# A block pair in fp32r on one core: the split weights get padded rows in place of two fixed offsets

## The reference

```python
h = modulate(rms_norm(x, pre_norm_mix), shift_m, scale_m)
o = attention(h @ w_in)                      # 2048 x 5656
x = x + gate_m * rms_norm(o @ w_o, post)     # 2048 x 2048
f = jnp.square(jax.nn.relu(h @ w_up)) @ w_down        # 2048 x 8192, 8192 x 2048
x = x + gate_f * rms_norm(f, post)
# second block: u @ w_in_2, three mixers, gates, branches, @ w_out_2, then
hdn = jnp.square(jax.nn.relu(_rms_norm(x, g) @ w_mlp_up))
x = x + _rms_norm(hdn @ w_mlp_down, post)
```

## Time and profile before

| | |
|---|---|
| median of 3 runs | 2995.68 us (2993.14 to 2997.9) |
| the profiled execution | 2997.9 us, span 2995.8 us |
| TensorE busy | 2902.8 us, 97% |
| VectorE busy | 1667.4 us, 56% |
| ScalarE busy | 1280.2 us, 43% |
| DMA | 596.72 MB, mean 199 GB/s |

### The profile page before, as it was taken

One profiled execution on the slowest core, in us unless ns is written; L12 is line 12 of the kernel. 1 busy time (PEld: TensorE's weight loads), 2 busy tenths in 40 slices (PEclk: granted clock), 3 DMA queues, 4 the chain that ended last, 5 costly groups with the idle time before them and its releaser, 6 DMA issues.

```text
span 2995.8 us, 50952 instructions
## 1 busy us (share of the span) xinstructions
PE 2902.8 (97%) x22340; PEld 2667.4 (89%) x22340; DVE 1667.4 (56%) x1484; ACT 1280.2 (43%) x1210; POOL 133.4 (4%) x111
## 2 busy tenths in 40 slices
PE   6999989999999999999999999999999999999999
PEld 5999987899889997889999789999978998899887
DVE  7878877794444454454455654444745444444444
ACT  3334444445334443346354444443344443344433
POOL 0011110000000000000022320000000000000000
PEclk8899999999999999999999999999999999999999
DMA  9998778596556655545451015556554555555553
GB/s 359 390 314 292 269 237 284 191 365 216 186 194 190 192 194 182 193 168 183 148 180 48 10 44 183 192 189 222 183 183 141 196 193 187 192 191 193 183 187 122
DMA packets 300452, 596.72 MB, mean 199 GB/s; under 512 B 12144, under 2 KB 17776, under 8 KB 299760
## 3 DMA queue, kind: packets, MB, share of 16 engines
q1 hardware_dynamic: 294864, 587.83, 58.1%
q10 hardware_dynamic: 5408, 6.23, 0.8%
HBM read 583.80 MB, written 6.29 MB: 197 GB/s over the span
## 4 chain that ended last, share of the span: by engine, by line
PE 86%; DVE 7%; ACT 3%; DMA 2%; issue 2%; POOL 0%; SPq 0%; ACTq 0%; DVEq 0%
PE ps L2275 32%; PE ps L2228 26%; PE ps L2791 9%; PE ps L2375 3%; PE ps L2390 3%; DVE ada_acc L1483 2%; PE ps L2912 2%; PE ps L2671 2%; DVE wL L1325 2%; ACT wH L765 1%; PE ps L2351 1%; DMA ada<-w_ada 1%; PE ps L2470 1%; ACT sqx L869 1%; PE ps L2252 1%
## 5 line engine op out<-in xcount | busy, mean ns | idle before, releaser
L1325 DVE TENSOR_TENSOR wL<-raw,wH 128x2048 fp32r<-128x2048 f32 x436 | 1004.3, 2304 | 1126.9 <-ACT wH L765 1122.5
L765 ACT ACTIVATE wH<-raw 128x2048 fp32r<-128x2048 f32 x436 | 837.3, 1920 | 1269.0 <-PE ps L2228 463.2
L2275 PE MATMUL ps<-actH,wH 128*128 128x256 f32 x2816 | 779.8, 277 | 2.9 <-DVE wL L1325 2.9
L2275 PE MATMUL ps<-actH,wL 128*128 128x256 f32 x2816 | 778.3, 276 | 0.0
L2275 PE MATMUL ps<-actL,wH 128*128 128x256 f32 x2816 | 778.3, 276 | 0.0
L2275 PEld LDWEIGHTS ps<-actH,wH 128*128 128x128 f32 x2816 | 529.5, 188 | 5.2 <-DVE wL L1325 3.3
L2275 PEld LDWEIGHTS ps<-actL,wH 128*128 128x128 f32 x2816 | 529.5, 188 | 0.1
L2275 PEld LDWEIGHTS ps<-actH,wL 128*128 128x128 f32 x2816 | 529.4, 188 | 0.0
L2228 PE MATMUL ps<-wL,hidH 128*128 128x512 f32 x1024 | 405.3, 396 | 0.0
L2228 PE MATMUL ps<-wH,hidH 128*128 128x512 f32 x1024 | 402.5, 393 | 1.3 <-DVE wL L1325 1.3
L2228 PE MATMUL ps<-wH,hidL 128*128 128x512 f32 x1024 | 401.0, 392 | 0.0
(11 more groups left out here) (419 smaller groups left out, 3681.5 us busy)
## 6 DMA issues: line engine op xcount, KB each, us to landing
raw<-w_in SPq DMA_DIRECT2D x96, 1024.0 KB, 5.2
ada<-w_ada SPq DMA_DIRECT2D x80, 1024.0 KB, 8.1
raw<-w_up SPq DMA_DIRECT2D x64, 1024.0 KB, 5.4
raw<-w_down SPq DMA_DIRECT2D x64, 1024.0 KB, 5.1
raw<-w_mlp_up SPq DMA_DIRECT2D x64, 1024.0 KB, 5.2
raw<-w_mlp_down SPq DMA_DIRECT2D x64, 1024.0 KB, 5.0
raw<-w_gates SPq DMA_DIRECT2D x48, 1024.0 KB, 5.1
raw<-w_o SPq DMA_DIRECT2D x16, 1024.0 KB, 6.2
```

The lines of the kernel that those rows point to most:

```text
L765: nc.scalar.activation(wH[:, s % SPLIT if L[name]["spg"] > 1 else r % SPLIT, :, :], raw[:, slot, :, :], ACT.Copy).then_inc(wh_ready, 1)
L1325: nc.vector.tensor_tensor(wL[:, b, :, :], raw[:, slot, :, :], wH[:, b, :, :].bitcast(F32), ALU.subtract).then_inc(wl_ready, 1)
L2275: ins = nc.tensor.matmul(out, w[:, b, k, cols], v[:, kk, :], start=(kk == 0 and j == 0 and n % 2 == 0), stop=(kk == STEP_K * spg - 1 and j ...
```

## The change

The two fixed offsets go. wH and wL get rows of `GC + PAD` = 516 elements, of which the first 512 are used: the rows of one block then lie 2064 bytes apart, not 2048. hidH, hidL, `o` and the scratch tiles behind it lie at whole KB from R0. Everything moves up by 96 bytes, and R0 is counted from the end of SBUF. Nothing else changes: instructions, their order, their waits and the bytes that they move are the same, but for the access patterns on wH and wL, which have four rows of 512 elements where there was one run of 2048.

```diff
-HIGH_AT, LOW_AT = 64, 192
+PAD = 4
...
-    top = [16512]
+    top = [16608]
...
     raw = new("raw", [P, RAW, STEP_K, GC])
-    top[0] += HIGH_AT
-    wH = new("wH", [P, SPLIT, STEP_K, GC], F32R)
-    top[0] += LOW_AT - HIGH_AT
-    wL = new("wL", [P, SPLIT, STEP_K, GC], F32R)
+    SPLIT0 = top[0]
+    wH = new("wH", [P, SPLIT, STEP_K, GC + PAD], F32R)[:, :, :, 0:GC]
+    wL = new("wL", [P, SPLIT, STEP_K, GC + PAD], F32R)[:, :, :, 0:GC]
...
-    R0 = ACT0 + 215 * 512
+    R0 = 229368 // 32 * 32 - 84 * 1024
...
-    hidH = at("hidH", [P, HT, T], F32R, R0 + HIGH_AT)
-    hidL = at("hidL", [P, HT, T], F32R, R0 + 32 * 1024 + LOW_AT)
-    o = at("o", [P, TT, D], F32, R0 + 64 * 1024 + LOW_AT)
+    hidH = at("hidH", [P, HT, T], F32R, R0)
+    hidL = at("hidL", [P, HT, T], F32R, R0 + 32 * 1024)
+    o = at("o", [P, TT, D], F32, R0 + 64 * 1024)
...
-    sqo = at("sqo", [P, TT, GC], F32, R0 + 80 * 1024 + LOW_AT)
+    sqo = at("sqo", [P, TT, GC], F32, R0 + 80 * 1024)
...
-    hid = at("hid_sq", [P, GT * T], F32, R0 + 80 * 1024 + LOW_AT)
+    hid = at("hid_sq", [P, GT * T], F32, R0 + 80 * 1024)
...
-    rtop[0] += LOW_AT
+    rtop[0] += 64 * PAD
```

## The result

| | before | after |
|---|---|---|
| median | 2996.51 us (2993.14 to 2997.9) | 3051.52 us (3044.9 to 3052.51, 4 runs) |
| profiled execution | 2997.9 us, span 2995.8 | 3041.57 us, span 3039.6 |

The ratio is 1.018, with a 95% interval of 1.0163 to 1.0198: the kernel is slower by 55 us. The forecast was no change, 2995 us, with 3025 as the upper end.

A forecast was written before the change was run, and what follows sets the result against it. TensorE's matmul pace was taken to bound the kernel. From the profiled 2997.9 us, -2.1 + 1.8 + 0 gave 2997.6, or 2995.4 on the median's scale; forecast 2995.0, no change, range 2963 to 3025.

The forecast's parts named there:

- What bounds the kernel: TensorE's matmul-to-matmul pace in the big-weight lines is the kernel's time: 2455 us of the 2996.
- VectorE and ScalarE at 0: The two splits per step, now four rows with gaps: a row break costs 0, and any cost is hidden.
- bound of 144 ns per row break: Splits on VectorE and ScalarE: a break costs at most an instruction start; three breaks 0.43 us, both engines 0.86.
- Transfers at 0: 1 MB loads land at another 256-byte phase; no cost in the sum, DMA share of the first 150 us unchanged.
- slower rival by transfers: DMA-full first 150 us: 2048-byte pieces may cost 96 bytes' worth more, 4.7%, +7 us, 3002; chance 0.05.
- Hidden activations at -2.1 us: Long matmuls with hidH and hidL stationary go from 231.1 to 230.4 ns, 3,072 of them: -2.1 us.
- The faster rival: 512-column matmuls lose their unevenness through 16-byte steps, all at 225 ns: -23 us, 2972; chance 0.26.
- Short matmuls at +1.8 us: 256-column matmuls: a third of 13,824 slow by 0.4 ns, the 0.3% of the nearest 512-column row: +1.8 us.
- The slower rival: 256-column matmuls slow where weights and activations share an address class: 4,608 at +4.4 ns, +20 us, 3015; chance 0.26.
- upper bound, +61 us: All short matmuls at 117.8 ns, the pace of the first ones behind a wait: +61 us, 3056.
- The sign in the profile after: L2275 pieces of 1536 at 177 us or more if the slower rival holds, more in wH products than wL.
- The rule on independent ports: TensorE has separate moving and weight-load read ports and never waits on another engine; by it distances are worth nothing.

The follow-up runs named there:

- e1: Kernel before with everything moved up by 96 bytes, distances between buffers unchanged: 2992.18 us against 2992.53, ratio 0.9999.
- e4: Kernel before with hidH and hidL alone moved to distance 0 from act: 2993.97 us, ratio 1.0004.
- e3: Kernel before with both offsets 0 and no padding, so wH, wL, hidH and hidL at distance 0 from act: 3057.71 us, ratio 1.0221.
- e8: Kernel before with wL and hidL moved to 64, so wH, wL, hidH and hidL all at 64: 3003.06 us, ratio 1.0036.
- e7: Kernel before with wL at distance 128 from act in place of 192, hidL kept at 192: 3055.21 us (one run) beside 2993.73.
- e2: Kernel before with only the wH and wL rows padded by 4 elements (16-byte steps), old offsets and base: 3053.82 us, ratio 1.021.
- e11: Kernel before with only a wait added ahead of up_1 and up2_1: 2992.21 us (one run), kernel before 2991.67.
- e9: Kernel before with hidL alone moved from 192 to 64: 2999.20 us against 2991.67, ratio 1.0023.
- e6: Kernel before with wL at distance 64 from act in place of 192, hidL kept at 192: 3014.19 us (one run) beside 2993.73.
- e10: e8 with a wait added ahead of up_1 and up2_1: 2993.58 us, ratio 1.0 to the kernel before.
- e5: Kernel before with wH and wL rows padded by one element (4-byte steps), old offsets: 3046.96 us (one run) against 2993.73.

## Why the prediction was wrong

- **What bounds the kernel: right.** TensorE's pace in the lines of the big matrices is its time, and the loss is made of 4.5 ns on each short matmul. TensorE's waits for a split stayed at 2.6 us ahead of L2274.
- **VectorE and ScalarE at 0: right.** The splits take 2306 and 1918 ns on four rows with gaps; before, the page has 2304 and 1920. The bound of 144 ns per row break was not needed.
- **Transfers at 0: right.** 1.01 and 1.03 busy at 356 and 380 GB/s in the first 150 us, and up_0 starts 0.5 us earlier than before. In e1 `raw` takes that phase of 224 with nothing padded, and the time is the same (0.9999): the slower rival by transfers did not happen.
- **Hidden activations at -2.1 us: right alone, not in the change.** Their move gives 230.4 ns (e4), but with stepping rows the long ones stay at 231.1 (177.49 us), so the term came out as 0. The faster rival, long ones at 225 ns through 16-byte steps, did not happen; what does bring them to 226.7 is distance 0 for all three products and no steps (e3, e8).
- **Short matmuls at +1.8 us: this is the step that failed.** I priced distances that no row showed by the nearest row, the 0.3% of the long form. The term took 0.4 ns on a third of the 13,824. The runs showed 4.5 ns, 4%, as the mean of all of them: 52.7 us on the 11,712 behind 560 us, of which 46.5 reach the chain. Two errors made that: the long form was taken to speak for the short one, while at distance 0 the one is fastest and the other slowest (e3); and 64 and 192 were read as two samples that see no sensitivity. They are the one sequence tried here that always falls to the fast pace; all at 0, wL at 128 and rows that step by 4 or 16 bytes hold it off, the last on most rows.
- **The slower rival: its place and its price for one matmul were right, its count was not.** Weights and activations at certain distances do slow the short stream, to about the 117.8 ns of the earlier trace rows. That this price fitted is not all luck: the nine matmuls behind a wait were the slow pace, seen before the stream fell out of it. The rival charged it to 4,608 matmuls (half the wH rows in two products), +20 us and 3015. e7 shows that one product at a bad distance slows all three, and e2 that good rows between bad ones are not clean. The prediction's upper bound, +61 us for all of them, 3056, was nearly the result of 3051.5. The range ended at 3025, short of a bound that the prediction had itself worked out for half of the span.
- **The sign in the profile after.** The prediction looked for more in the wH products than in the wL one. It rose in all of them (281, 281, 280 ns); e7 shows the same, one bad product slowing all three.
- **The rule on independent ports.** The prediction set the Trainium skill, "SBUF — State Buffer", section "Who interferes with whom", beside the rows: two independent read ports, and TensorE never waits on another engine. No run here shows TensorE waiting for another engine on account of an address, and its pace in e3 is 120.0 ns with VectorE and ScalarE busy or idle, so on that the trace agrees. Taken as far as the prediction took it, that distances between its two operands are worth nothing, the measurements decide against it: 113.4, 118.2 and 120.0 ns for the same instructions.

What is open: why the pace follows the distance. That it is counted modulo 256 is my measure and not shown: in every layout without stepping rows wH and wL lie a whole multiple of 512 bytes plus the given distance behind actH and actL, so the short stream never told 256 and 512 apart. Distances like 16, 32 or 48 were never tried without stepping rows. And actH and actL lie in one class, so that the short stream can't tell whether the distance to a matmul's own weights counts or that to the weights loaded for the next. Whether the moving read and the weight load of the next matmul meet in one place of SBUF, or whether it is something else, no run here tells. Nor is it shown which property of the entry picks the pace at 64 and 64. That front parts differ by some us between kernels with one pace of the short matmuls or nearly so, which hides gains of 5 us, is seen (the first x768 starts at 741.82 to 748.76 in before, e1, e4 and e8 to e11) and not explained.

## What to carry to other kernels

Where a stream of matmuls sets the time, its pace can hang on the addresses of both operands; measure it from a long stretch divided by its count, before and after anything that moves a buffer, padding of rows above all. Don't price an untested layout by another form of the same instruction; where no row covers the layout that half of the span will have, the range has to reach to the bound. If a stream runs above its best pace, try the other offsets below 256 bytes and a gap ahead of it, one at a time.

## What the runs showed of the hardware

At the 2.4 GHz level, for fp32r matmuls with a weight load each. Distances are those of the three products in their order in the stream:

| form | distances | ns each | seen in |
|---|---|---|---|
| 256 columns | 64, 64, 192 | 113.4 | before, e1, e4, e9, e11 |
| 256 columns | 64, 64, 64 | 113.4 or 117.8 | e6, e8, e10 |
| 256 columns | 64, 64, 128 | 118.2 | e7 |
| 256 columns | 0, 0, 0 | 120.0 | e3 |
| 256 columns | steps of 16 or 4 bytes | 117.9 to 118.3 | after, e2, e5 |
| 512 columns | 0, 0, 0 | 226.7 | e3, e8, e10 |
| 512 columns | 64, 64, 64 | 229.0 | e6, e8, e10 (x336, on actH and actL) |
| 512 columns | 64, 192, 64 | 230.4 | e4; before (x336) |
| 512 columns | 0, 128, 128 | 231.1 | before, e1, e11 |
| 512 columns | 0, 0, 128 and 0, 64, 128 | 231.1 | e6; e7 (its x624 pieces 232.6) |
| 512 columns | steps of 16 or 4 bytes | 231.1 to 231.9 | after, e2, e5 |
| 512 columns | 0, 128, 0 | 233.3, once 231.5 | e9 |

Two things in it I had not expected. A stream can hold either of two paces over 1536 matmuls with nothing different but its entry, 180.91 against 174.34 us. And the best distances of one form, all at 0 with 512 columns, are the worst of the other.
